# The last row tile of w_ada as TensorE weights in two chunks of the head

## The chip, the cores and the metric

The kernel runs on one core of one Trainium2 chip. The metric is the device time of one launch, in microseconds (us); less is better.

## The reference, cut to what matters

The program is one decoder block on 256 tokens of width 2048, float32 throughout. Before anything else it needs the conditioning vector's projection:

```python
mod = (jax.nn.silu(c) @ w_ada[l] + b_ada[l])[:, None, :]
sh1, sc1, gt1, sh2, sc2, gt2 = jnp.split(mod, 6, axis=-1)
h = rmsnorm(x, g_pre_mix[l]) * (1.0 + sc1) + sh1
y = hybrid_mixer(h, ...)            # h @ w_in, attention heads and recurrent heads, @ w_out
x = x + gt1 * rmsnorm(y, g_post_mix[l])
h = rmsnorm(x, g_pre_ffn[l]) * (1.0 + sc2) + sh2
y = hier_moe(h, ...)                # 32 experts of three 2048 x 512 matrices each
x = x + gt2 * rmsnorm(y, g_post_ffn[l])
```

`c` is one row of 2048 numbers and `w_ada` is 2048 x 12288, so this is a vector times a matrix: all of the matrix is read, and each number is used once. The head of the kernel needs the first two of the six parts, shift `sh1` and scale `sc1`, before `h` exists.

## The kernel before, in words

**The head.** The 2048 columns of shift and scale are cut into five chunks of 4, 4, 4, 2 and 2 tiles of 128 (`CHUNKS`, line 93). A chunk holds the same column tiles of shift and of scale, so a chunk of 4 tiles is 1024 numbers wide. Its 16 row tiles of 128 rows come in four pieces `("head", c, r)` of four row tiles each, and each piece in four transfers: two for its first two row tiles (semaphore `landed`), two for its last two (semaphore `rest_landed`), sent by the SP queue (SyncE) in `head` (from line 370, the DMA itself on line 380). After each chunk's four pieces SP sends blocks of `w_in` (`first`, through `send`, line 361). SP sends in a fixed order written out by hand and waits, in that order, until the ring slot that a piece goes into is free.

**Chunk 0** is done by TensorE as a row product (line 578). **Chunks 1 to 4** are done by VectorE: `head_piece` (from line 1671) runs through the 16 row tiles of the chunk, and for each it does `sum = w_row_tile * silu(c)_tile + sum`, the first on line 1686 and the other 15 on line 1688. The sum is 128 partitions by 1024 (512 for chunks 3 and 4) and still has to be summed over the partitions. After the last piece it raises `part_ready`.

**TensorE's part** is `head_columns(c)`: after `mod_copied` for the chunk before, it issues constant products on fixed data whose result is never read (line 585: 16 in chunk 1, 8 in chunk 2, none in 3 and 4), waits for `part_ready`, and multiplies each 128 x 128 tile of the sum, as weights, with a column of ones (line 598), 8 narrow products for a chunk of 4 tiles, into 8 columns of PSUM bank 7. ScalarE copies these columns to `mod` (line 1287), VectorE makes the affine numbers (lines 1729 to 1731), and VectorE and ScalarE apply them to the chunk's tiles of `hT` (lines 1733 and 1291).

**The order around it.** TensorE is in order. It takes `hT` tile by tile (k = 0 to 15) and multiplies it with 15 column tiles of `w_in` (line 641). Within the last k of chunk c, after 8 of the 15 tiles (1 for chunk 2's last k), it runs `head_columns(c + 1)`. So chunk 1's columns stand inside k = 3, and chunk 2's inside k = 7; the 7 tiles behind them cover the trip through ScalarE and VectorE before k = 4 or k = 8 starts. A slot of the ring is given free by VectorE after it has read a piece (`free` in `head_piece`), and SP may then send the next into it.

**Behind the head** come the rest of the input projection, the recurrent heads, attention, the output projection, the routing, and from about 615 us on the experts, whose weights stream through the ring to the end.

In the profile a float32 product has two rows for each matmul, so 8 narrow products are x16 and 16 constant ones are x32.

Of the kernel before, what the change touches and what calls it, by code (L numbers as in the profile page):

```python
# [34 lines left out]
P = 128  # L35
D = 2048
S = 256
TT = S // P
KT = D // P
# [49 lines left out]
TRANSFERS = [[2 if name[0] == "head" else 1 for name in names] for names in SLOT_LOADS]  # L89
PLACE = {name: (slot, n) for slot, names in enumerate(SLOT_LOADS) for n, name in enumerate(names)}  # L90
HEAD_TILES = 15
IN_ORDER = 16
CHUNKS = [(0, 4), (4, 4), (8, 4), (12, 2), (14, 2)]
BY_DVE = [k0 + i for k0, n in CHUNKS for i in range(n // 2)]
# [84 lines left out]
def block_kernel(nc, a, out):  # L179
# [3 lines left out]
    with ExitStack() as ctx:  # L183
# [5 lines left out]
        def sig(name):  # L189

            if name in STAGE_OF:
                stages, n = STAGE_OF[name]
                counted = sig(stages)
                assert counted.n == n - 1, name
                return counted
            if name not in sems:
                sems[name] = Signal(ctx.enter_context(nc.semaphore(name)))
            return sems[name]

        def wait(eng, name, n=1):  # L200

            if name in STAGE_OF:
                name, n = STAGE_OF[name]
            eng.wait_ge(sig(name).sem, n)
# [20 lines left out]
        silv = sb("silv", [P, KT])  # L225
# [82 lines left out]
        bank = [ctx.enter_context(nc.psum_tensor(f"bank{i}", [P, BLK], F32)) for i in range(8)]  # L308
# [16 lines left out]
        def landed(eng, name):  # L325

            s, n = PLACE[name]
            eng.wait_ge(sig(f"landed{s}").sem, 16 * sum(TRANSFERS[s][0:n + 1]))

        def free(ins, name):  # L330

            ins.then_inc(sig(f"freed{PLACE[name][0]}").sem, 1)
# [17 lines left out]
        def rows_of(name, k, n):  # L350
            return flat(name)[:, 0:k * n].rearrange("p (k c) -> p k c", k=k)
# [3 lines left out]
        def _(sp):  # L355
# [27 lines left out]
            def first(q, h):  # L383
                send(("first", q, h), win_k[:, 4 * q + 2 * h:4 * q + 2 * h + 2, HEAD_COL:HEAD_COL + HEAD_TILES * P])

# [130 lines left out]
            for e in range(2, NE - 2):  # L516
                if e < IN_ORDER:
                    first_halves(e, e % 2)
                for s in range(2, HB):
                    next_piece(e + 1, s, e)  # L520
                if e >= IN_ORDER:
                    first_halves(e, e % 2)
# [25 lines left out]
        def _(pe):  # L548
            mm = nc.tensor.matmul
# [32 lines left out]
            def constant_products(n, first_chunk=False):  # L582

                for _ in range(n):
                    mm(bank[0 if first_chunk else 7][:, S + 64:2 * S], ident, cst[:, C_UP:C_UP + 192], start=first_chunk, stop=True,
                       skip_group_check=True)

            def head_columns(c):

                k0, n = CHUNKS[c]  # L590
                if c > 0:
                    wait(pe, "mod_copied", c)
                    constant_products((16, 8, 0, 0)[c - 1])
                pe.wait_ge(sig("part_ready").sem, c + 1)
                if c == 0:
                    wait(pe, "shift_row")
                for j in range(2 * n):
                    last = mm(bank[7][:, S + 2 * k0 + j:S + 2 * k0 + j + 1], head_sums[c % 2][:, j * P:(j + 1) * P], ones[:, 0:1], start=c == 0, stop=True,
                              skip_group_check=True)
                last.then_inc(sig("column_sums").sem, 1)  # L600

            def late_row(w, out):
# [20 lines left out]
            for c in range(5):  # L623
                k0, nk = CHUNKS[c]
                for k in range(k0, k0 + nk):
                    q, h = k // 4, k % 4 // 2
# [4 lines left out]
                    if k % 2 == 0:  # L631
                        landed(pe, ("first", q, h))
                    w = rows_of(("first", q, h), 2, HEAD_TILES * P)
                    tiles = list(range(HEAD_TILES))
                    if k == KT - 1:
                        tiles = tiles[7:] + tiles[:7]
                    for n, t in enumerate(tiles):
                        if c < 4 and k == k0 + nk - 1 and n == (8, 8, 1, 8)[c]:
                            head_columns(c + 1)
                        half_ = bank[(t - 1) // 2][:, (t - 1) % 2 * S:((t - 1) % 2 + 1) * S] if t else bank[7][:, 0:S]  # L640
                        last = mm(half_, w[:, k % 2, t * P:(t + 1) * P], hT[:, k, :],  # L641
                                  start=k == 0 and (t == 0 or t % 2 == 1), stop=k == KT - 1, skip_group_check=True)
                        if k == KT - 1 and t == HEAD_TILES - 1:
                            last.then_inc(sig("forget_full").sem, 1)
# [5 lines left out]
            for r in range(4):  # L650
                for j in range(4):
                    k = 4 * r + j
                    last = mm(bank[4][32 * j:32 * j + 32, 0:S], wg24[:, k, :], hT[:, k, :], start=r == 0, stop=r == 3,
                              skip_group_check=True)
# [3 lines left out]
            for k in range(KT):  # L658
                last = mm(bank[3][:, 0:S], rows_of("hq", KT, P)[:, k, :], hT[:, k, :], start=k == 0, stop=k == KT - 1)
# [131 lines left out]
            for v, name in enumerate(("w1k", "w1v")):  # L791
# [3 lines left out]
                for r in range(8):  # L795
                    for j in range(4):
                        q = 4 * r + j
                        last = mm(bank[3][32 * j:32 * j + 32, v * P:(v + 1) * P], blkv[:, q, :], rows_of(name, CMP_LEN, P)[:, q, :],
                                  start=r == 0, stop=r == 7, skip_group_check=True)
# [4 lines left out]
            for v in range(2):  # L804
                c0, n = (256, 32) if v == 0 else (288, 160)
                last = mm(bank[3][:, c0:c0 + n], cpart[:, v * P:(v + 1) * P], cst[:, C_SUM:C_SUM + n], start=True, stop=True)
# [4 lines left out]
            last = mm(bank[3][:, 448:480], w2[:, 0, :], cmph[:, 0, 0:32], start=True, stop=True)  # L811
            for g in range(KVG):
                last = mm(bank[3][:, g * P:(g + 1) * P], cmph[:, 1, 16 * g:16 * g + P], w2[:, 1, :], start=True, stop=True)
# [65 lines left out]
            for tt in range(TT):  # L879
                for h in range(NH):  # L880
                    o = bank[3 + 2 * tt + h // 4][:, (h % 4) * P:(h % 4 + 1) * P]
                    for jt in range(tt + 1):
                        aT = at[:, h, tt * P:(tt + 1) * P] if jt == 0 else at[:, h, S:S + P]
                        last = mm(o, aT, htok[:, h // 4, jt, (h % 4) * P:(h % 4 + 1) * P], start=jt == 0, stop=jt == tt)
# [8 lines left out]
            for g in range(KVG):  # L893
                for tt in range(TT):
                    last = tr(bank[1][:, (2 * g + tt) * P:(2 * g + tt + 1) * P], pcp[:, tt, g * P:(g + 1) * P], ident)
# [96 lines left out]
            for tt in range(TT):  # L992
                for m in range(4):
                    wait(pe, "rec_gated", tt * NH + 4 * (m // 2) + 4)
                    for j in range(2):
                        h = 2 * m + j
                        last = tr(bank[OUT_BANKS[2 + tt][m // 2]][:, (m % 2) * 256 + j * P:(m % 2) * 256 + (j + 1) * P],
                                  orec[:, tt, h * P:(h + 1) * P], ident)
# [34 lines left out]
            for m in range(3):  # L1033
                for k in range(4 * m, 4 * m + 4):
                    mm(bank[GB[m]][:, (k % 4) * P:(k % 4 + 1) * P], x_t[:, 0, k * P:(k + 1) * P], onehot[:, 0, :],
                       start=k % 4 == 0, stop=False, skip_group_check=True)
# [9 lines left out]
            last = mm(bank[3][:, 32:64], cst[:, C_UP:C_UP + P], sel[:, 1, :], start=False, stop=True)  # L1046
# [17 lines left out]
            for m in range(3):  # L1064
                for k in range(4 * m, 4 * m + 4):
                    last = mm(bank[GB[m]][:, (k % 4) * P:(k % 4 + 1) * P], x_t[:, 1, k * P:(k + 1) * P], onehot[:, 1, :],
                              start=False, stop=True, skip_group_check=True)
# [143 lines left out]
            with pe.If(over > 0):  # L1211
# [4 lines left out]
                for tt in range(TT):  # L1216
                    for c in range(4):
# [4 lines left out]
                        for j in range(4):  # L1222
                            k = 4 * c + j
                            last = tr(bank[2 + i % 2][:, j * P:(j + 1) * P], x_t[:, tt, k * P:(k + 1) * P], ident)
# [3 lines left out]
                with pe.Fori(0, NE) as e:  # L1228
                    pe.wait_ge(sig("dense_here").sem, e + 1)
                    for tt in range(TT):  # L1230
                        c = e * 2 + tt
                        for s in range(2):
                            for k in range(KT):
                                last = mm(bank[s][:, :], h2T[:, k, tt * P:(tt + 1) * P], ring[:, 2 * (k // 8) + s, k % 8, :],
                                          start=k == 0, stop=k == KT - 1)
                        last.then_inc(sig("dense_gu").sem, 1)
                        pe.wait_ge(sig("dense_hid").sem, c + 1)
                        for f in range(4):
                            last = tr(bank[2][:, f * P:(f + 1) * P], dhid[:, f:4 * P:4], ident)
                        last.then_inc(sig("dense_T").sem, 1)  # L1240
                        pe.wait_ge(sig("dense_T_copied").sem, c + 1)
                        for n in range(4):
                            for k in range(4):
                                wdn = ring[:, 4 + k // 2, :, :].rearrange("p (k a) b -> p k (a b)", k=2)[:, k % 2, :]
                                last = mm(bank[4 + n][:, :], dhidT[:, k * P:(k + 1) * P], wdn[:, n * BLK:(n + 1) * BLK],
                                          start=k == 0, stop=k == 3)
# [412 lines left out]
        def _(dve):  # L1659
# [13 lines left out]
            def head_piece(q, r):  # L1673

                n = 2 * CHUNKS[q][1] * P
                acc_q = head_sums[q % 2][:, 0:n]
                if r == 0 and q > 1:
                    wait(dve, "column_sums", q - 1)
                landed(dve, ("head", q, r))
                w = rows_of(("head", q, r), 4, n)  # L1680
                for k in range(4):
                    if k == 2:
                        wait(dve, f"rest_landed{r}", 32 * (q + 1))
                    c = silv[:, 4 * r + k:4 * r + k + 1]
                    if r == 0 and k == 0:
                        ins = ts(acc_q, w[:, k, :], c, None, ALU.mult)
                    else:
                        ins = stt(acc_q, w[:, k, :], c, acc_q, ALU.mult, ALU.add)
                    if k < 3:
                        step(ins)  # L1690
                    else:
                        free(ins, ("head", q, r))
                        used(dve, ("head", q, r))
                if r == 3:
                    dve.sem_inc(sig("part_ready").sem, 1)
# [271 lines left out]
            for h in range(NH):  # L1967
# [5 lines left out]
                for br in range(2):  # L1973
                    for tt in range(TT):
                        c0, n = (0, P) if tt == 0 else (P, 2 * P)
                        w = probs[:, h % 2, br, c0:c0 + n]
# [17 lines left out]
            for tt in range(TT):  # L1994
                for h in range(NH):
                    n = tt * NH + h
# [241 lines left out]
            with dve.If(over > 0):  # L2238
                for tt in range(TT):
                    ts(x_t[:, tt, :], x_t[:, tt, :], rstd2[:, tt:tt + 1], None, ALU.mult).then_inc(sig("dense_x").sem, 1)  # L2240
                for i in range(8):
                    wait(dve, "dense_xT", i + 1)
                    for j in range(4):
                        k = 4 * (i % 4) + j
# [3 lines left out]
                with dve.Fori(0, NE) as e:  # L2248
                    for tt in range(TT):
                        c = e * 2 + tt  # L2250
# [6 lines left out]
                        for n in range(4):  # L2257
                            w = ysum[:, tt, n * BLK:(n + 1) * BLK]
# [19 lines left out]
            for i in range(8):  # L2278
                dve.wait_ge(sig("scattered").sem, 8 * (NE // 2 - 1) + i + 1)
                c0 = LAST_COLS[i % 4] * BLK  # L2280
                w = ysum[:, i // 4, c0:c0 + BLK]
# [56 lines left out]
```

## Time and profile before

| | |
|---|---|
| median of 3 runs | 1557.26 us (1556.84 to 1557.4) |
| profiled execution, its own time | 1559.59 us |
| its span, first to last instruction | 1557.7 us |
| TensorE busy | 1510.4 us (97%) |
| VectorE busy | 682.2 us (44%) |
| ScalarE busy | 231.6 us (15%) |
| bytes moved, rate over the span | 589.96 MB, 379 GB/s |
| mean granted TensorE clock | 0.995 |

TensorE counts as busy from a matmul's start to its modelled end, so a busy share near 100% says that it was never without an instruction, not that it ran at its peak. The span is 1.9 us shorter than the execution's own time, and that execution is 2.33 us above the median of the runs.

### The profile page before, as it was taken

What the parts mean: (1) busy time and instruction counts of PE and PEld (TensorE: products, weight loads), DVE (VectorE), ACT (ScalarE), POOL (GpSimd) and SP (SyncE); (2) the same over time, 40 slices, a digit from 0 to 9 for tenths busy, and PEclk for the clock granted to TensorE, in tenths of its full rate; (3) what the DMA queues carried; (4) which work ended last, traced back from release to release, by engine and by line L of the source; (5) the groups of instructions that cost most, each with busy time, mean ns of one, the idle gap of its engine ahead of it and who ended that gap; (6) DMA issues with size and microseconds to landing.
All of it is one profiled execution on the core that took longest, in us unless ns stands there. A gap on an engine that the chain in (4) does not pass through costs nothing.

```text
span 1557.7 us, 19266 instructions
## 1 busy us (share of the span) xinstructions
PE 1510.4 (97%) x7980; PEld 811.0 (52%) x7980; DVE 682.2 (44%) x1228; ACT 231.6 (15%) x443; POOL 41.4 (3%) x57
## 2 busy tenths in 40 slices
PE   5999999999999999999999999999999999999996
PEld 2888888855654446444434434434434434434432
DVE  3574767776887636232332332332332322322325
ACT  2100311121322303011010010011010011010003
POOL 1001000000001200000000000000000000000003
PEclk9999999999999999999999999999999999999998
DMA  9999677799878996899999999999999999999993
GB/s 361 397 385 365 259 270 271 280 359 352 305 289 319 364 387 269 364 427 427 428 429 427 429 429 427 429 428 429 398 423 429 428 428 429 428 428 429 427 429 164
DMA packets 102802, 589.96 MB, mean 379 GB/s; under 512 B 6224, under 2 KB 16944, under 8 KB 77408
## 3 DMA queue, kind: packets, MB, share of 16 engines
q1 hardware_dynamic: 100384, 580.93, 91.9%
q0 software_dynamic: 1696, 5.66, 1.1%
q10 hardware_dynamic: 672, 2.66, 0.4%
q8 instruction: 36, 0.59, 0.2%
q14 instruction: 14, 0.11, 0.0%
HBM read 587.07 MB, written 2.16 MB: 378 GB/s over the span
## 4 chain that ended last, share of the span: by engine, by line
PE 66%; DMA 25%; SPq 5%; DVE 2%; issue 1%; ACTq 0%; ACT 0%; DVEq 0%
DMA ring<-in_w_up 22%; PE bank L1165 21%; PE bank L925 7%; PE bank L1198 7%; PE bank L675 5%; SPq L380 5%; PE bank L1079 4%; PE bank L641 4%; PE bank L866 4%; PE bank L1059 3%; PE bank L709 2%; DMA ring<-in_w_ada 2%; PE bank L688 1%; PE bank L691 1%; DMA ring<-in_w_in 1%; PE bank L1090 1%
## 5 line engine op out<-in xcount | busy, mean ns | idle before, releaser
L1165 PE MATMUL bank<-ring,RN 128*64 128x512 f32 x1488 | 330.9, 593 | 9.4 <-DMA ring<-in_w_up 9.4
L1165 PEld LDWEIGHTS bank<-ring,RN 128*64 128x64 f32 x1488 | 106.5, 137 | 223.1 <-issue 199.0
L1198 PE MATMUL bank<-ring,RN 128*64 128x512 f32 x992 | 219.7, 595 | 0.5 <-issue 0.5
L2216 DVE TENSOR_TENSOR RN<-bank,RN 64x512 f32<-64x512 f32 x31 | 21.5, 693 | 376.1 <-ACT RN L1519 376.1
L1198 PEld LDWEIGHTS bank<-ring,RN 128*64 128x64 f32 x992 | 68.9, 137 | 137.4 <-issue 135.6
L2223 DVE COPY RG<-bank 64x512 f32<-64x512 f32 x64 | 44.1, 689 | 196.1 <-PE bank L1198 188.4
L1059 PEld LDWEIGHTS bank<-RN,RX 128*128 128x128 f32 x976 | 111.5, 192 | 13.0 <-issue 13.0
L1059 PE MATMUL bank<-RN,RX 128*128 128x128 f32 x976 | 115.7, 277 | 0.0
L925 PE MATMUL bank<-ring,RT 128*128 128x512 f32 x256 | 113.0, 596 | 0.8 <-DVE RT L2003 0.8
L1165 PE MATMUL bank<-RT,RN 128*64 128x512 f32 x256 | 112.3, 592 | 0.0
L1079 PE MATMUL bank<-RG,RN 128*128 128x512 f32 x240 | 109.5, 599 | 0.0
L2152 DVE TENSOR_SCALAR RN<-bank,aff 128x128 f32<-128x128 f32 x256 | 87.2, 403 | 43.0 <-PE bank L1059 41.1
L1165 PE MATMUL bank<-RH,RN 128*64 128x512 f32 x240 | 105.4, 592 | 0.0
L2189 DVE TENSOR_TENSOR RT<-RT,bank 128x512 f32<-128x512 f32 x112 | 75.7, 687 | 20.5 <-PE bank L1079 18.6
L675 PE MATMUL bank<-RH,ring 128*128 128x256 f32 x384 | 84.0, 380 | 0.0
L1712 DVE SCALAR_TENSOR_TENSOR wide<-ring,silv,wide 128x1024 f32<-128x1024 f32 x60 | 77.0, 1283 | 8.3 <-DMA ring<-in_w_ada 6.5
L675 PEld LDWEIGHTS bank<-RH,ring 128*128 128x128 f32 x384 | 72.6, 190 | 9.9
L1533 ACT ACTIVATE RG<-bank 64x512 f32<-64x512 f32 x64 | 37.9, 592 | 265.5 <-PE bank L1198 259.1
L925 PEld LDWEIGHTS bank<-ring,RT 128*128 128x128 f32 x256 | 47.5, 190 | 57.2 <-issue 56.1
L1519 ACT ACTIVATE RN<-bank 64x512 f32<-64x512 f32 x31 | 18.3, 589 | 391.0 <-PE bank L1165 391.0
L1165 PEld LDWEIGHTS bank<-RT,RN 128*64 128x64 f32 x256 | 35.1, 137 | 72.2 <-issue 72.2
L1079 PEld LDWEIGHTS bank<-RG,RN 128*128 128x128 f32 x240 | 43.4, 191 | 55.2 <-issue 51.6
(395 smaller groups left out, 1472.6 us busy)
## 6 DMA issues: line engine op xcount, KB each, us to landing
ring<-in_w_down SPq DMA_DIRECT2D x64, 2048.0 KB, 15.5
ring<-in_w_up SPq DMA_DIRECT2D x48, 2048.0 KB, 20.9
ring<-in_w_gate SPq DMA_DIRECT2D x47, 2048.0 KB, 17.3
ring<-in_w_ada SPq DMA_DIRECT2D x32, 2048.0 KB, 10.5
ring<-in_w_in SPq DMA_DIRECT2D x18, 2048.0 KB, 9.2
RT<-in_w_gate SPq DMA_DIRECT2D x17, 2048.0 KB, 15.5
RH<-in_w_up SPq DMA_DIRECT2D x16, 2048.0 KB, 20.0
ring<-in_w_ada SPq DMA_DIRECT2D x48, 512.0 KB, 11.6
```

The source lines that it names most:

```text
L380: sp.dma_start(dst[:, j0:j1, m * w:(m + 1) * w], ada_k[:, 4 * r + j0:4 * r + j1, m * D + k0 * P:m * D + k0 * P + w]).then_inc(sig(landing) ...
L641: last = mm(half_, w[:, k % 2, t * P:(t + 1) * P], hT[:, k, :], start=k == 0 and (t == 0 or t % 2 == 1), stop=k == KT - 1, skip_group_chec ...
L675: last = mm(bank[PAIR[name][m // 2]][:, (m % 2) * S:(m % 2 + 1) * S], w[:, m * P:(m + 1) * P], hT[:, k, :], start=k == 0 and m % 2 == 0, s ...
L866: last = mm(bank[2][:, :], hT[:, k, tt * P:(tt + 1) * P], rows_of((name, k // 8), 8, BLK)[:, k % 8, :], start=k == 0, stop=k == KT - 1)
L925: last = mm(bank[OUT_BANKS[n][tt]][:, :], mixed(k)[:, tt * P:(tt + 1) * P], rows_of(("out", n, h), 8, BLK)[:, k % 8, :], start=k == 0, sto ...
L1059: last = mm(bank[GB[m % 3]][:, (k % 4) * P:(k % 4 + 1) * P], x_t[:, tt, k * P:(k + 1) * P], onehot[:, tt, :], start=tt == 0, stop=tt == TT ...
L1079: mm(bank[4 + i % 4][:, :], ohwT[:, tt * P:(tt + 1) * P], rows[:, c * BLK:(c + 1) * BLK], start=True, stop=True).then_inc(sig("scattered") ...
L1165: last = mm(bank[0][64 * s:64 * s + 64, :], tokT[:, k, q * CAP:(q + 1) * CAP], w[:, k % 8, :], start=k == 0, stop=k == KT - 1, skip_group_ ...
L1198: last = mm(bank[2 + n % 2][64 * (n // 2):64 * (n // 2) + 64, :], hidT[:, k * CAP:(k + 1) * CAP], wdn[:, n * BLK:(n + 1) * BLK], start=k = ...
L1712: ins = stt(acc_w, w[:, k, :], c, acc_w, ALU.mult, ALU.add)
L2152: ins = ts(tokT[:, k, :], bank[GB[m % 3]][:, (k % 4) * P:(k % 4 + 1) * P], aff[:, 2, k:k + 1], aff[:, 3, k:k + 1], ALU.mult, ALU.add)
L2189: ins = v.tensor_copy(w, bank[4 + i % 4][:, :]) if first else tt_op(w, w, bank[4 + i % 4][:, :], ALU.add)
```

## The change

In `head_columns` of chunks 1 and 2, TensorE takes the last row tile (row tile 15) of the chunk's eight column tiles straight from the ring as weights, with column 15 of `silu(c)` moving: 8 narrow products into the same 8 columns of bank 7, before the products of the sum with ones, which accumulate onto them. VectorE leaves out its step for that row tile in these chunks. The constant products go from 16 to 10 in chunk 1 and from 8 to 3 in chunk 2. TensorE now waits for the landing of the last piece before it waits for `part_ready`, and it is TensorE's first product of the sum that gives slot 3 free, no longer VectorE. Nothing else is changed.

```diff
+LAST_ROWS_PE = (1, 2)
...
                 if c > 0:
                     wait(pe, "mod_copied", c)
-                    constant_products((16, 8, 0, 0)[c - 1])
+                    constant_products((10, 3, 0, 0)[c - 1])
+                if c in LAST_ROWS_PE:
+                    landed(pe, ("head", c, 3))
+                    wait(pe, "rest_landed3", 32 * (c + 1))
+                    w = rows_of(("head", c, 3), 4, 2 * n * P)
+                    for j in range(2 * n):
+                        mm(bank[7][:, S + 2 * k0 + j:S + 2 * k0 + j + 1], w[:, 3, j * P:(j + 1) * P], silv[:, KT - 1:KT], start=False, stop=True,
+                           skip_group_check=True)
                 pe.wait_ge(sig("part_ready").sem, c + 1)
...
                 for j in range(2 * n):
                     last = mm(bank[7][:, S + 2 * k0 + j:S + 2 * k0 + j + 1], head_sums[c % 2][:, j * P:(j + 1) * P], ones[:, 0:1], start=c == 0, stop=True,
                               skip_group_check=True)
+                    if c in LAST_ROWS_PE and j == 0:
+                        free(last, ("head", c, 3))
...
-                for k in range(4):
+                for k in range(3 if r == 3 and q in LAST_ROWS_PE else 4):
```

## Rows read from the trace of the kernel before

**Rows 1.** Busy tenths of TensorE and DMA in 40 slices, from the page
```profile
PE   5999999999999999999999999999999999999996
...
DMA  9999677799878996899999999999999999999993
```
**Rows 2.** Chain that ended last, experts: start us, us, what
```profile
830.52 21.87 DMA ring<-in_w_up
852.43 7.14 PE bank L1165 x32
```
**Rows 3.** Stretches: length, busy us of each engine (instructions), clock, DMA share, GB/s
```profile
200.00:300.00 100.00, 100.00 (x1043) 86.91 (x1042) 72.37 (x68) 17.20 (x15) 0.00 (x0) 1.00 0.76 282
...
620.00:640.00 20.00, 18.04 (x93) 7.38 (x91) 6.75 (x26) 0.97 (x2) 0.00 (x0) 1.00 0.71 290
```
**Rows 4.** Timeline of TensorE, 28 to 112 us: start us, us, what
```profile
36.36 1.84 PE L598 MATMUL bank<-ones,wide 128*128 128x1 f32 x16
38.06 1.22 PE L585 MATMUL bank<-cst 128*128 128x192 f32 x6
...
62.38 5.36 PE L585 MATMUL bank<-cst 128*128 128x192 f32 x32
68.38 1.95 PE L598 MATMUL bank<-ones,RN 128*128 128x1 f32 x16 [0.63 <-DVEq L1695]
70.19 3.27 PE L641 MATMUL bank<-RH,RT 128*128 128x256 f32 x14
...
96.17 2.76 PE L585 MATMUL bank<-cst 128*128 128x192 f32 x16
99.44 1.95 PE L598 MATMUL bank<-ones,wide 128*128 128x1 f32 x16 [0.51 <-DVEq L1695]
```
**Rows 5.** Timeline of VectorE, 28 to 160 us
```profile
49.49 18.78 DVE L1688 SCALAR_TENSOR_TENSOR RN<-ring,silv,RN 128x1024 f32<-128x1024 f32 x14 [0.64 <-DMA ring<-in_w_ada]
...
80.52 18.81 DVE L1688 SCALAR_TENSOR_TENSOR wide<-ring,silv,wide 128x1024 f32<-128x1024 f32 x14 [0.61 <-DMA ring<-in_w_ada]
...
127.31 11.78 DVE L1688 SCALAR_TENSOR_TENSOR wide<-ring,silv,wide 128x512 f32<-128x512 f32 x15
```
**Rows 6.** Chain that ended last, 30 to 170 us
```profile
53.04 2.57 SPq L380
...
85.25 11.38 DMA ring<-in_w_ada
...
96.73 1.29 DVE wide L1688
...
98.05 1.30 DVE wide L1688
...
124.38 0.79 PE bank L598 x8
...
141.24 0.79 PE bank L598 x8
```
**Rows 7.** DMA issues at 53.0 to 53.5 us: KB, us to landing
```profile
ring<-in_w_ada SPq DMA_DIRECT2D x1, 512.0 KB, 12.5
```
**Rows 8.** DMA issues at 85.5 to 87 us, and SP's timeline there
```profile
RT<-in_w_in SPq DMA_DIRECT2D x1, 1920.0 KB, 14.8
...
86.53 2.58 SPq L361 DMA_DIRECT2D RT<-in_w_in  x2
```
**Rows 9.** Chain that ended last, behind the head
```profile
304.02 13.93 DMA ring<-in_w_ada
```
**Rows 10.** TensorE's timeline, and stretches with its clock (third number from the right)
```profile
22.70 3.64 PE L578 MATMUL bank<-ring,RN 128*32 128x512 f32 x16 [4.00 <-DMA ring<-in_w_ada]
...
21.00:22.00 1.00, 0.00 (x0) 0.00 (x0) 0.25 (x2) 0.60 (x2) 0.00 (x0) 0.94 1.06 389
...
28.00:29.00 1.00, 1.00 (x8) 1.00 (x7) 0.69 (x1) 0.03 (x1) 0.00 (x0) 0.65 1.05 385
...
68.38:70.33 1.95, 1.95 (x17) 1.95 (x18) 0.00 (x0) 0.00 (x0) 0.00 (x0) 1.00 0.99 410
```

## The prediction

> **What bounds the kernel now.** I began with the page's slices. TensorE shows nine tenths in all but the first and the last slice [rows 1], so I asked which parts of that are held up by something else. The DMA engines are also near full, except in nine of the slices 5 to 17. The two long stages therefore have different limits. In the experts the chain alternates: a transfer of 21.87 us, 7.14 us of TensorE, and again [rows 2]. That stage runs as fast as the weights come, and its end is fixed by when it could begin. Between the head and the experts TensorE is the limit: from 200 to 300 us it is busy 100.00 of 100 us, with the DMA engines at 0.76 [rows 3]. The last stretch where the DMA engines are clearly not full is 620 to 640 us, at 0.71 [rows 3]. So whatever TensorE gains in the head should reach the start of the experts' streaming, as long as nothing in between waits for something that did not move.
>
> Next I read the head in TensorE's timeline. Two idle times are put down to VectorE's last step, 0.63 us before chunk 1's narrow products at 68.38 and 0.51 us before chunk 2's at 99.44 [rows 4]. Ahead of each stand the constant products, 5.36 us and 2.76 us, whose results nobody reads. So TensorE stands for about 6.0 and 3.3 us per chunk waiting or filling, and only VectorE's end (chunk 1), or the landing of the last rows plus two VectorE steps (chunk 2), sets when it may go on. In the chain, chunk 2 is plain: the transfer issued at 85.25 takes 11.38 us and lands at 96.63, VectorE takes its last two row tiles from 96.73 and 98.05, and TensorE follows at 99.44 [rows 4, 6].
>
> **The change, part by part.**
>
> *VectorE, one step less.* Fourteen steps take 18.78 us in chunk 1 [rows 5], 1.34 us each with the gap. The last ended at 68.27, and without it the sum is ready at 66.93. TensorE started 0.11 us after VectorE's end before, so it may start at 67.04. In chunk 2 the step at 98.05 goes [rows 6]. The one at 96.73 stays, since it waits for the landing, and ends at 98.02; with the same lag TensorE may start at 98.13.
>
> *TensorE, chunk 1.* A constant product costs 5.36 / 16 = 0.335 us [rows 4]. Ten end at 62.38 + 3.35 = 65.73. Then come the two added waits for the landing. The last transfer of the piece was issued at 53.04 [rows 6] and took 12.5 us [rows 7], so it landed at 65.54, just before. Eight narrow products with weights from the ring are not in the trace. The nearest rows are the eight with ones, of the same shape: 36.36 to 38.06 is 1.70 us, 68.38 to 70.19 is 1.81 us [rows 4]. I take 1.75, since both are rows of just this form. That gives 67.48 for the first product of the sum. This is later than VectorE's 67.04, so TensorE's own work is now the bound and the idle time is gone. Before it was 68.38: **0.90 us gained**. With 1.81 us and 0.1 us for the two waits it is 0.74, with 1.70 it is 0.95.
>
> *A rule against the row.* The row gives 1.70 / 8 = 0.21 us for one narrow product. The Trainium skill, "TensorE: Matmul & The Clock Gate", section "Back-to-back issue gap", gives about 60 cycles for a free size of 1 to 64, 25 ns; as an estimate by that page the 16 rows of eight products would be 0.4 us, and chunk 1 would then be bound by VectorE's 67.04 and gain 1.34 us. The row has the duration, and I use it.
>
> *TensorE, chunk 2.* Its constant products start 0.90 us earlier, at 95.27. Three cost 3 x 2.76 / 8 = 1.04 us [rows 4], to 96.31. The last rows land at 96.63 whatever TensorE does: the DMA queue is full at this time and the transfer was issued at 85.25, so neither the sooner sum nor the later freeing of slot 3 moves it. TensorE waits until about 96.7, as VectorE does. Plus 1.75 is 98.45, later than VectorE's 98.13. Before it was 99.44: **0.99 us gained in all**, not on top of chunk 1. In other words, what followed the landing was two VectorE steps in a row, and is now eight narrow products beside one step. With 1.81 and 0.1 for waits it is 0.83. If the landing came some tenths earlier with the lighter traffic, it would be 1.1.
>
> *The freeing of slot 3.* It moves from VectorE's end, 68.27, to about 67.7, and in chunk 2 from 99.35 to about 98.7. SP sent the next piece's last transfers around 85 [rows 6], far behind the first of these, so nobody waits. I cost it at nothing; its cover is 17 us in chunk 1.
>
> *What must give way behind it.* Chunk 4's VectorE sum ends at 139.09 [rows 5] and TensorE takes it at 141.24 [rows 6]: 2.15 us of slack, and part of VectorE's chain moves up with the columns. For chunk 3 the chain shows TensorE following its own work at 124.38 with no VectorE step ahead [rows 6]. The block of `w_in` for k = 8 is issued at 86.53 and takes 14.8 us [rows 8], landing at 101.33, and TensorE needs it when the seven tiles behind chunk 2's columns are done, 3.27 us by the same seven tiles at 70.19 [rows 4], so at 103.5 even after the move: it covers a move of 1 us. After 160 us nothing but TensorE is on the chain until a transfer issued at 304.02 [rows 9], which TensorE's products release. It moves with them.
>
> *Sum.* -0.99 us at 101 us, carried through. The profiled execution would go from 1559.59 to 1558.6. That execution is 2.33 us above the median of the runs, so the median goes from 1557.26 to 1556.3, or 0.06%.
>
> **The rivals.**
>
> *A: the gain is given back.* If a transfer sent early in a full queue, or the experts' rhythm, is the true clock of the end, then the 1 us becomes idle time. For it: the DMA engines are full in the head and from 640 us on. Against it: 0.76 from 200 to 300 and 0.71 at 620 to 640 [rows 3]; a queue that is empty there cannot carry an old limit through. Time 1557.3.
>
> *B: the clock falls (the slower side).* TensorE's clock went down once early: in an idle time of 4.00 us it fell within 21 to 22 us (granted 0.94 over that stretch), and it came back within 28 to 29 (0.65) [rows 10]. That is some 6.8 us at 1.2 GHz instead of 2.4, worth 3.4 us of TensorE's time at most. Now each chunk has 16 narrow products in a row, some 3.5 us, in which the weight loads are busy but one column moves. If these were taken for idleness, the clock would fall behind chunk 1's columns, in k = 3 and 4. The price is -0.99 + 3.4 = +2.4 for one fall, 1559.7, and -0.99 + 6.8 = +5.8 for one in each chunk, 1563.1. It decides once the stretch of narrow products is long enough, and the longest seen, 1.95 us at 68.38 right behind 0.63 us of idleness, ran at 1.00 [rows 10]. It is now less than twice that, with the idleness gone. The Trainium skill, same page, section "What's actually happening", says the default state is the throttled one and activity releases it, and it leaves open whether such products count. No row here shows 3.5 us of them.
>
> *C: the columns do not move.* If the last rows in fact land so late in chunk 2 that TensorE waits for them and then does narrow products that cost more from the ring, say 2.6 us as two VectorE steps did, nothing is gained: 1557.3. Against it: the form is the same, and both operands lie in SBUF before and after.
>
> **How the numbers follow.** Two tenths of a per cent, 3.1 us, is about what a measurement of this kernel can tell from no change. Chances: forecast 0.79, A 0.09, C 0.02, one fall of the clock 0.04, two falls 0.03, something unseen on the fast side 0.03. Faster by over 0.2% would need 3.1 us, and all filling and waiting that the two chunks lose is 5.9 us less 3.5 us of new products, so it takes something unseen: 0.03. Slower by over 0.2% is the two falls: 0.03. Within: the other four cases, 0.94. The range: the bounds of the gain are 0.83 and 1.1, which gives 1556.2 to 1556.4. The three runs differ by 0.56 us, which I allow on either side, and the same again below, as the experts' rhythm may lock in slightly better: 1555.2. Above it takes in A and C with the same spread: 1558.0.
>
> **What would show it.** Right: chunk 1's narrow products are 32 rows from about 65.8 with no idle time before the second half; in chunk 2 a short wait for a transfer, from 96.3 to 96.7, the sum's products near 98.45, and the k behind them about 1.0 us earlier; the transfer at 304.02 about 1.0 us earlier; and the experts' rows earlier by as much. Wrong: a clock under 1.00 between 66 and 110 us (B); an idle time of TensorE between 100 and 620 us that grew by 1 us (A); narrow products from the ring that take clearly over 1.8 us for eight (C).

## The result: 0.14% slower, where 0.06% faster was forecast

| | before | changed |
|---|---|---|
| median of the runs | 1557.57 us (20 runs, 1555.97 to 1559.37) | 1559.70 us (20 runs, 1554.94 to 1564.23) |
| ratio | | 1.0014, interval 1.0008 to 1.0020 |
| profiled execution, span | 1559.59, 1557.7 us | 1559.61, 1557.8 us |

The two profiled executions took the same time, and the two sets of runs did not. The changed kernel also spreads more than twice as wide: 9.3 us against 3.4.

TensorE's timeline of the changed kernel (start us, us, what); the rows answer to [rows 4]:

```profile
62.18 3.41 PE L586 MATMUL bank<-cst 128*128 128x192 f32 x20
65.43 1.84 PE L600 MATMUL bank<-silv,ring 128*128 128x1 f32 x16
67.13 1.93 PE L606 MATMUL bank<-ones,RN 128*128 128x1 f32 x16
68.92 4.95 PE L651 MATMUL bank<-RH,RT 128*128 128x256 f32 x14
73.71 23.04 PE L651 MATMUL bank<-RH,ring 128*128 128x256 f32 x106
96.59 1.14 PE L586 MATMUL bank<-cst 128*128 128x192 f32 x6
97.56 1.84 PE L600 MATMUL bank<-silv,ring 128*128 128x1 f32 x16
99.27 3.08 PE L606 MATMUL bank<-ones,wide 128*128 128x1 f32 x16
102.21 5.44 PE L651 MATMUL bank<-RH,ring 128*128 128x256 f32 x14
107.49 20.02 PE L651 MATMUL bank<-RH,RT 128*128 128x256 f32 x92
```

In chunk 1 the plan worked: from the start of the constant products to the first product of the sum it is 67.13 - 62.18 = 4.95 us, and it was 68.38 - 62.38 = 6.00. Both idle times are gone. But the seven tiles behind (x14) take 4.95 us against 3.27 before, and in chunk 2 the eight products of the sum take 3.08 us against 1.95 and the seven tiles 5.44 against 3.27. The same instructions take longer. The stretches of the changed kernel say why; the third number from the right is the granted clock, and the two figures after the length are TensorE's matmul and weight-load time:

```profile
66.00:68.00 2.00, 2.00 (x20) 2.00 (x20) 0.41 (x1) 0.00 (x0) 0.00 (x0) 1.00 0.98 407
68.00:70.00 2.00, 2.00 (x13) 1.82 (x13) 0.63 (x4) 0.41 (x2) 0.00 (x0) 0.77 1.00 415
70.00:72.00 2.00, 2.00 (x6) 1.53 (x6) 0.92 (x5) 1.98 (x3) 0.00 (x0) 0.50 1.01 411
72.00:74.00 2.00, 2.00 (x10) 1.72 (x9) 0.00 (x0) 1.96 (x4) 0.00 (x0) 0.88 1.01 389
...
98.00:100.00 2.00, 2.00 (x19) 2.00 (x18) 0.00 (x0) 0.00 (x0) 0.00 (x0) 0.95 1.02 422
100.00:102.00 2.00, 2.00 (x11) 2.00 (x11) 0.00 (x0) 0.00 (x0) 0.00 (x0) 0.50 1.02 422
104.00:106.00 2.00, 2.00 (x6) 1.58 (x5) 0.00 (x0) 0.15 (x1) 0.00 (x0) 0.50 1.08 356
```

Clock 0.50 of 2.4 GHz is the 1.2 GHz level. In chunk 1 it fell behind the 16 narrow products, in chunk 2 among them, and there with matmuls and weight loads both busy in 2.00 of 2.00 us. The kernel before ran at 1.00 in the same places:

```profile
66.00:70.00 4.00, 3.37 (x26) 3.07 (x24) 2.23 (x2) 0.00 (x0) 0.00 (x0) 1.00 1.00 415
70.00:74.00 4.00, 4.00 (x21) 3.56 (x22) 1.54 (x8) 3.09 (x6) 0.00 (x0) 1.00 1.01 403
98.00:102.00 4.00, 3.49 (x26) 3.12 (x25) 1.62 (x5) 0.18 (x1) 0.00 (x0) 1.00 1.02 424
102.00:106.00 4.00, 4.00 (x20) 3.54 (x19) 0.80 (x3) 1.09 (x2) 0.00 (x0) 1.00 1.03 371
```

The time that it cost: the tiles from k = 8 on start at 107.49, 3.13 us later than in the kernel before, whose row is

```profile
104.36 7.93 PE L641 MATMUL bank<-RH,RT 128*128 128x256 f32 x36
```

The first transfer on the chain behind the head is as late, 307.16 against 304.02 [rows 9]. At the start of the experts 2.75 us are left; one wait for a transfer of `w_in` at 353 us is 0.40 us shorter than before and takes up that much. Two rows of the changed kernel's chain of waits (start us, us, what):

```profile
307.16 13.63 DMA ring<-in_w_ada
...
618.69 2.68 PE bank L1076 x24
```

and the second of them in the kernel before:

```profile
615.94 2.68 PE bank L1066 x24
```

That the two spans end alike all the same is due to the stretch behind. From this row to the end of the span the kernel before took 941.8 us in its profiled execution, which was 2.33 us over the median, and the changed one 939.1. The profiles of the experiments below speak for the second: ten of the fourteen, the changed kernel's among them, took 938.8 to 939.7 us here, with starts from 614.98 to 620.33. So the profile of the kernel before is the unusual one. Why its experts took 2.7 us longer stays open.

So the end of one pair of profiles can't carry the comparison, and the start of the experts carries it better: 2.75 us late there, and 2.1 us at the median.

A second measure is the mean granted clock that every run reports. In 105 runs of the kernel before, made beside the experiments below, it averages 0.9959 (median 1557.69 us), and in the 20 runs of the changed kernel 0.9935. The difference, 0.0024 x 1557 = 3.7 us, is what TensorE would lose if all of it fell where TensorE is the limit. The mean does not say where the clock fell, and places outside the head are in it, as the last section shows. It tells how much of this there was, and not what it cost.

### The profile page after: what moved, and what is told of

It is laid out like the page before. It is cut to its first block, busy times and chain, and to the rows that moved or that the text cites. A ratio compares the mean times of both kernels' runs of the same rounds, so it can differ in the third digit from the quotient of the medians.

```text
span 1557.8 us, 19286 instructions
## 1 busy us (share of the span) xinstructions
PE 1514.3 (97%) x7990; PEld 815.1 (52%) x7990; DVE 679.6 (44%) x1226; ACT 231.6 (15%) x443; POOL 41.3 (3%) x57
## 4 chain that ended last, share of the span: by engine, by line
PE 77%; DMA 20%; DVE 2%; issue 0%; SPq 0%; ACTq 0%; ACT 0%; DVEq 0%
PE bank L1175 22%; DMA ring<-in_w_up 17%; PE bank L1208 9%; PE bank L935 7%; PE bank L651 7%; PE bank L685 5%; PE bank L1069 4%; PE bank L1089 4%; PE bank L876 4%; DMA ring<-in_w_ada 2%; PE bank L719 2%; PE bank L698 1%; PE bank L701 1%; DMA ring<-in_w_in 1%; PE bank L1100 1%; PE bank L842 1%
```

## Experiments

Each kernel was run beside the kernel before. "Clock" is the mean over its runs of each run's mean granted clock. The averages of 11 or 12 runs are uncertain by some 0.0005. In the profiled execution with four tiles between, the clock falls only at the very end, where TensorE is done, and its mean is 0.998.

| kernel | runs | median us | ratio to before, interval | clock |
|---|---|---|---|---|
| before | 105 | 1557.69 | | 0.9959 |
| changed | 20 | 1559.70 | 1.0014 (1.0008 to 1.0020) | 0.9935 |
| all constant products kept | 5 | 1562.93 | 1.0041 (1.0028 to 1.0054) | 0.9940 |
| spare narrow products | 11 | 1560.82 | 1.0017 (1.0008 to 1.0027) | 0.9934 |
| 3 constant products between | 6 | 1561.66 | 1.0026 (1.0014 to 1.0037) | 0.9930 |
| 3 tiles between | 12 | 1557.22 | 1.0005 (0.9994 to 1.0017) | 0.9951 |
| before, fewer constant products | 11 | 1559.13 | 1.0008 (0.9999 to 1.0017) | 0.9938 |
| change in chunk 1 alone | 11 | 1558.32 | 1.0006 (0.9997 to 1.0015) | 0.9950 |
| change in chunk 2 alone | 11 | 1559.26 | 1.0009 (1.0001 to 1.0018) | 0.9946 |
| groups of four | 12 | 1559.52 | 1.0018 (1.0008 to 1.0027) | 0.9942 |
| 4 tiles between | 12 | 1556.97 | 0.9999 (0.9991 to 1.0008) | 0.9959 |
| chunk 2 alone, 4 tiles between | 11 | 1556.20 | 0.9994 (0.9985 to 1.0003) | 0.9956 |
| the same again | 12 | 1556.68 | 0.9993 (0.9984 to 1.0001) | 0.9964 |
| before, columns later | 11 | 1558.05 | 1.0004 (0.9995 to 1.0013) | 0.9942 |

### Is it the constant products that were taken away?

```diff
-                    constant_products((10, 3, 0, 0)[c - 1])
+                    constant_products((16, 8, 0, 0)[c - 1])
```

> The changed kernel with all 16 and 8 constant products kept. Theory N (16 narrow products in a row are what lets the clock fall): the granted clock is 0.5 for some us behind chunk 1's or chunk 2's columns here too, and the time is over that of the changed kernel's full-clock case by the five to six extra products and up to 5 us: 1559 to 1564 us, ratio to before 1.001 to 1.003. Theory F (the missing constant products are what lets it fall): clock 1.00 from 60 to 110 us, the sum's columns in chunk 1 start at 62.3 + 5.4 + 1.7 = 69.4 against 68.4 before, so 1 to 2 us slower than before and no more, with mean clocks as before (0.995 or above).

Measured: 1562.93 us, clock 0.9940. With every constant product in place the clock still fell. In the profiled execution it stayed up behind chunk 1 and went down behind chunk 2, as these stretches show (columns as above):

```profile
102.00:104.00 2.00, 2.00 (x16) 1.86 (x16) 0.42 (x4) 0.20 (x2) 0.00 (x0) 0.93 1.00 394
104.00:106.00 2.00, 2.00 (x6) 1.64 (x5) 0.72 (x2) 1.08 (x2) 0.00 (x0) 0.50 1.05 348
```

Theory F alone is out, since it had the clock at 1.00 throughout. The median is within N's 1559 to 1564 us, the ratio above N's 1.003. These are five runs.

### Is it the ring as the source of weights, or what VectorE no longer does?

```diff
+                if c in (1, 2):
+                    for j in range(2 * n):
+                        mm(bank[7][:, S + 2 * KT + j:S + 2 * KT + j + 1], ident, ones[:, 0:1], start=False, stop=True,
+                           skip_group_check=True)
```

> The kernel before with 10 and 3 constant products and then eight narrow products of an identity tile with a column of ones into unused columns; VectorE does all its steps, and nothing reads the ring for the new products. Theory N or F: the clock falls as in the changed kernel (0.5 behind chunk 1 or 2), and the time is about 1 us above the changed kernel, 1560 to 1562 us median, mean clocks 0.992 to 0.994. Theory W (weights from the ring, or the moving column of silu, have to do with it): clock 1.00 at 60 to 110 us and a time within 1 us of before, since TensorE only fills idle time.

Measured: 1560.82 us, clock 0.9934, the changed kernel's 0.9935. TensorE's stream is that of the changed kernel but for 0.35 us of idleness in chunk 1, and nothing is gained from it. Theory W is out: eight narrow products on fixed data are enough. The median is 1.1 us above the changed kernel's, but runs that range over 7 to 9 us in both don't show this difference (the ratios are 1.0017 and 1.0014), so it is no measure of what the useful part of the change brings.

### Is it 16 narrow products in a row?

```diff
-                    constant_products((10, 3, 0, 0)[c - 1])
+                    constant_products((7, 0, 0, 0)[c - 1])
...
+                    constant_products(3)
                 pe.wait_ge(sig("part_ready").sem, c + 1)
```

> The changed kernel with the same number of constant products, but three of them between the two groups of narrow ones (7+3 and 0+3). Theory N: the clock stays at 1.00 from 60 to 110 us; the sum's columns start at about 68.1 and 99.3, so the time is within 0.5 us of before, and mean clocks are as before. Theory F: the clock falls as in the changed kernel, 1559 to 1562 us.

Measured: 1561.66 us, clock 0.9930. The clock fell behind both chunks in the profiled execution; one stretch behind each:

```profile
70.00:72.00 2.00, 2.00 (x9) 1.63 (x9) 1.25 (x7) 1.06 (x3) 0.00 (x0) 0.60 0.98 400
...
102.00:104.00 2.00, 2.00 (x9) 2.00 (x10) 0.06 (x1) 0.18 (x1) 0.00 (x0) 0.50 0.99 391
```

The longest row of narrow products here is eight, as before. Theory N is out as worded. In chunk 1 TensorE was also idle for 0.64 us ahead of the first group; in chunk 2 it was not idle at all, so idleness is not needed for the fall.

### Real work between the two groups

`head_columns` is cut in two; the sum's part is called three tiles later.

```diff
+                        if c < 4 and k == k0 + nk - 1 and n == (11, 11, 1, 8)[c]:
+                            head_sum_columns(c + 1)
```

> The changed kernel with the sum's columns three tiles of w_in later (after 11 of 15 tiles and not after 8), so that real work stands between the two groups of narrow products. Theory N: clock 1.00 from 60 to 110 us, the sum's columns of chunk 2 start at 99.7 and k = 8 about 1.1 us earlier than before: ratio 0.9985 to 1.000, median about 1556.5 us. Theory F: the clock falls still, and it is not faster than before.

Measured: 1557.22 us, clock 0.9951. The median is 2.5 us under the changed kernel's, and by the ratio it is no faster than before: four of its 12 runs took over 1560 us, the other eight 1555.37 to 1558.38. In the profiled execution the clock held behind chunk 1 and fell in chunk 2, where TensorE had come early with its three constant products and was idle before the narrow ones, as its timeline shows:

```profile
96.46 2.20 PE L601 MATMUL bank<-silv,ring 128*128 128x1 f32 x16 [0.63 <-DMA ring<-in_w_ada]
98.53 2.91 PE L659 MATMUL bank<-RH,ring 128*128 128x256 f32 x6
```

This neither bears out N nor F. It led to theory L: idleness and narrow products count alike.

### Idleness in place of narrow products

```diff
-                    constant_products((16, 8, 0, 0)[c - 1])
+                    constant_products((10, 3, 0, 0)[c - 1])
```

This is the kernel before, with no product added.

> The kernel before with 10 and 3 constant products and nothing else changed: TensorE is idle for about 2.6 and 2.1 us ahead of the sum's eight narrow products, and idle plus narrow make some 4.5 us with hardly a column moved. Theory L (what lets the clock fall is a stretch with few columns moved, be it idleness or narrow products): the clock falls about as often as in the changed kernel, mean clock near 0.9935, median 1559 to 1561 us. Theory N (only narrow products in a row, 1.95 us here as before): mean clock 0.996 as before and the median within 0.5 us of before.

Measured: 1559.13 us, clock 0.9938, nearly that of the changed kernel. TensorE was idle 2.94 us and then did eight narrow products, and the clock fell there. TensorE's timeline:

```profile
68.48 3.37 PE L598 MATMUL bank<-ones,RN 128*128 128x1 f32 x16 [2.94 <-DVEq L1695]
```

and the stretch behind:

```profile
70.00:74.00 4.00, 4.00 (x15) 3.55 (x16) 1.54 (x8) 1.59 (x4) 0.00 (x0) 0.50 0.99 393
```

As L has it. It also shows what the constant products are for: nobody reads their results, and with 11 fewer of them the mean clock is lower and the median 1.4 us higher. The ratio's interval begins at 0.9999, so the clock is shown and the time only likely.

### One chunk alone

`LAST_ROWS_PE = (1,)` with constant products (10, 8), and `(2,)` with (16, 3).

> The change in chunk 1 alone. Theory L: falls behind chunk 1 in most runs, none more than before behind chunk 2; mean clock 0.9945 to 0.995, median 0.5 to 2 us above before. If the falls cost nothing, the gain of chunk 1 alone is 0, since chunk 2 then waits for the same landing: median as before.

Measured: 1558.32 us, clock 0.9950.

> The change in chunk 2 alone. Theory L: falls behind chunk 2 in most runs, mean clock 0.9945 to 0.995, median 0.5 to 2 us above before; in runs of mean clock 0.997 or more, about 0.5 us less than before, since TensorE now goes on from the landing after one VectorE step. Without a cost of the clock, the median would be 0.3 to 0.5 us under before.

Measured: 1559.26 us, clock 0.9946. In either profiled execution the clock fell behind the changed chunk alone. The losses of clock, 0.0009 and 0.0013, add up to 0.0022, against 0.0024 for both, so either chunk has a share of about half, as far as averages this uncertain can tell. The two best runs of the second took 1555.70 and 1556.60 us at a clock of 0.996, where the 33 runs of the kernel before with this clock average 1558.04; two runs are no more than a hint of the gain.

### Four groups of four, with a tile between

The 16 products stand in four groups after tiles 8, 9, 10 and 11, with 10 and 5 constant products ahead.

```diff
+                        if c < 2 and k == k0 + nk - 1 and n in range(8, 12):
+                            narrow_step(c + 1, n - 8)
```

> The changed kernel with the 16 narrow products of a chunk in four groups of four, with one tile of w_in (0.43 us of full-width work) between any two, and 10 and 5 constant products. TensorE's work is the same but for two products. Theory L: a stretch of 3.4 us now holds 1 us or more of full-width work, against none in the changed kernel, so the clock falls seldom: mean clock 0.996, median 1.0 to 1.4 us under before (1556.4 to 1556.8), ratio about 0.9992. Theory C (the clock falls by some chance that has nothing to do with how the narrow products stand): mean clock 0.9935 and slower than before by 1 to 3 us.

Measured: 1559.52 us, clock 0.9942. A miss for L with the measure that I had put to it: with a tile of full-width work between any two groups of four the mean clock was nearly that of the changed kernel, and far from the 0.996 expected. The last groups of chunk 1 and what followed, in TensorE's timeline:

```profile
67.81 0.68 PE L675 MATMUL bank<-RH,RT 128*128 128x256 f32 x2
68.32 0.95 PE L605 MATMUL bank<-ones,RN 128*128 128x1 f32 x8
69.13 0.68 PE L675 MATMUL bank<-RH,RT 128*128 128x256 f32 x2
69.64 1.09 PE L605 MATMUL bank<-ones,RN 128*128 128x1 f32 x8
70.60 3.51 PE L675 MATMUL bank<-RH,RT 128*128 128x256 f32 x8
```

and the stretch with the clock:

```profile
70.00:72.00 2.00, 2.00 (x9) 1.75 (x9) 0.94 (x5) 0.73 (x3) 0.00 (x0) 0.58 1.00 407
```

The four tiles at 70.60 took 3.51 us; the same tiles at full clock take 1.97.

### Two groups, four tiles apart and next to no idleness

The sum's part stands after 12 tiles instead of 8, with 10 and 5 constant products.

> The changed kernel with four tiles of w_in (1.74 us) between the two groups of narrow products and 10 and 5 constant products, so that TensorE is not idle while it waits for chunk 2's last rows. Theory L (the clock falls when a stretch with few columns moved is long): each narrow group of 1.75 us now has full-width work on both sides, less than the 0.6 us of idleness and 1.95 us of narrow products of before; mean clock 0.9955 or more, median 1556.6 to 1557.2 us, 0.5 to 1.2 under before. Theory T (it is the total of narrow products near each other that counts, however parted within 6 us): mean clock 0.994 to 0.995 as in the variant with four groups of four, 1558 to 1560 us.

Measured: 1556.97 us, clock 0.9959, that of the kernel before. In the profiled execution the clock did not fall in the head at all; one of the 12 runs had 0.992 and took 1561.64 us, so falls are rarer here, and not gone. TensorE's timeline at chunk 1:

```profile
65.61 1.92 PE L601 MATMUL bank<-silv,ring 128*128 128x1 f32 x16 [0.20 <-DMA ring<-in_w_ada]
67.39 1.97 PE L659 MATMUL bank<-RH,RT 128*128 128x256 f32 x8
69.20 1.84 PE L611 MATMUL bank<-ones,RN 128*128 128x1 f32 x16
70.90 1.54 PE L659 MATMUL bank<-RH,RT 128*128 128x256 f32 x6
```

and the two stretches with their clock:

```profile
66.00:70.00 4.00, 4.00 (x30) 3.79 (x30) 0.86 (x1) 0.00 (x0) 0.00 (x0) 1.00 1.02 424
98.00:102.00 4.00, 4.00 (x31) 3.79 (x30) 0.00 (x0) 0.00 (x0) 0.00 (x0) 1.00 1.02 422
```

TensorE does the same 16 narrow products here as in the changed kernel, and the median is 2.7 us lower. Theory T's clock and time are both missed. The three tiles left behind the sums, 1.54 us, cover the way through ScalarE and VectorE: k = 4 follows at 72.28 with no idle time. What the change was to gain is seen here, since the clock is out of the way. Work on k = 8 starts 0.93 us before the 104.36 of the kernel before:

```profile
103.43 8.84 PE L659 MATMUL bank<-RH,RT 128*128 128x256 f32 x40
```

and the experts' first row on the chain starts 0.96 us earlier, at 614.98 against 615.94. At the medians of the runs this gain does not show: the ratio is 0.9999, with 0.9991 to 1.0008.

### Chunk 2 alone, four tiles apart

Chunk 1 is as before. Chunk 2 has 2 constant products, the narrow group on the last row tile, four tiles, the sum's group and three tiles.

> The change in chunk 2 alone, 2 constant products there and four tiles of w_in between the two narrow groups; chunk 1 as before with 16. Theory L: mean clock 0.9955 or more and median 0.3 to 1.0 us under before (1556.7 to 1557.4), since the wait for chunk 2's landing is what the gain hangs on. Theory T: a fall behind chunk 2 in half of the runs, mean clock about 0.995, and the median at or above before.

Measured: 1556.20 us, ratio 0.9994 (0.9985 to 1.0003), clock 0.9956. This is the best version, and it was run once more:

> The same kernel as the variant with the change in chunk 2 alone and four tiles between its narrow groups, for a second interval. If its gain is real, the ratio is again 0.9990 to 0.9998 and the median about 0.9 us (0.3 to 1.5) under before, with a mean clock of 0.9955 to 0.9965; if the first interval was luck, the ratio is 1.0000 to 1.0006.

Measured: 1556.68 us, ratio 0.9993 (0.9984 to 1.0001), clock 0.9964. Over both, 23 runs have a median of 1556.65 us, 1.0 under before's 1557.69. It beats the changed kernel clearly. Against the kernel before, both ratios lie in the expected range, but each interval still reaches 1, so a gain of 0.06% is likely and not proved. In both profiled executions the clock fell behind chunk 1, whose code is before's, and the seven tiles there took 4.96 us: so the kernel before has such falls too, at times.

### Only the order changed, in the kernel before

```diff
-                        if c < 4 and k == k0 + nk - 1 and n == (8, 8, 1, 8)[c]:
+                        if c < 4 and k == k0 + nk - 1 and n == (11, 11, 1, 8)[c]:
```

with 12 constant products for 16 in chunk 1.

> The kernel before, nothing taken from VectorE, with the chunk's narrow products after 11 of 15 tiles instead of 8 in chunks 1 and 2, and 12 constant products for 16 in chunk 1 (8 in chunk 2 as before): three tiles of real work stand ahead of VectorE's end and not behind it. No narrow product is added, so under L and T alike the clock does as before (0.996). The four tiles left behind the columns, 1.74 us, cover the 1.1 us through ScalarE and VectorE. Expected 1.3 us earlier at k = 8, median 1556.2 to 1556.6 us, ratio 0.9990 to 0.9996. If the four tiles do not cover it, or the fewer constant products cost clock, as before or slower.

Measured: 1558.05 us, clock 0.9942: a miss. Three tiles did come ahead of VectorE's end, but the mean clock is lower (0.9942, where the runs of before beside it had 0.9961), with no narrow product added. In chunk 2 of the profiled execution TensorE was idle 0.87 us and the four tiles behind took 3.16 us in place of 1.97, by its timeline:

```profile
99.17 1.95 PE L598 MATMUL bank<-ones,wide 128*128 128x1 f32 x16 [0.87 <-DVEq L1695]
100.97 3.16 PE L641 MATMUL bank<-RH,ring 128*128 128x256 f32 x8
```

## Why the prediction was wrong

**VectorE, one step less: right.** In chunk 1 its 13 steps end at 66.42 in the changed kernel, before TensorE's 67.13, and TensorE no longer waits.

**TensorE, chunk 1: right.** Eight narrow products with weights from the ring start 1.70 us ahead of the next group (65.43 to 67.13); I had taken 1.75. From the start of the constant products chunk 1 gained 1.05 us, with 0.90 forecast. The estimate by the Trainium skill, "TensorE: Matmul & The Clock Gate", section "Back-to-back issue gap", 0.4 us for the eight, was off by four times. The same section says that this gap is a matmul's by itself, and that it comes out too small at small free sizes where each matmul has a weight load; I had left that out. Here each of the 16 rows has a weight load (192 ns on average in the changed kernel's profile, each overlapping the next), and the rows follow each other every 0.106 us.

**TensorE, chunk 2: right, but not seen in the changed kernel.** There TensorE came late from chunk 1's fall of the clock, began the narrow products at 97.56 and had no landing to wait for. With three tiles between, where it came early, it waited 0.63 us for the transfer and went on at 96.46; I had taken about 96.7.

**The freeing of slot 3: nobody waited**, as costed. The last rows of chunk 2 had landed before TensorE came to them at 97.56.

**The sum, "carried through": right as a mechanism.** With four tiles between, where the clock held in the profiled execution, k = 8 came 0.93 us earlier and the experts 0.96 us, with 0.99 forecast, and from there on ten profiles took the same time within 1 us. The changed kernel's 3.13 us at k = 8 came through as 2.75. So rival A (given back) has at most these 0.4 us for it. At the medians the gain itself is not shown: no ratio below 1 has an interval that leaves 1 out. The one run of the changed kernel with a mean clock of 0.998 took 1554.94 us, the lowest of its 20. Rival C (dear narrow products) is out by the 1.70 us.

**The step that failed is the price of narrow products**, which I took for their own 1.75 us only; the sum has no term for the clock. I gave rival B, the fall of the clock, 7 in 100, and dismissed it with one row: 0.63 us of idleness and 1.95 us of narrow products had run at 1.00 [rows 10]. Three things were wrong in this. One execution shows one outcome of something that varies from run to run: before's 105 runs range from 0.994 to 0.998 in mean clock, and two profiles of code that is before's in chunk 1 show the fall that its own profile lacks. The row was the most that had been shown to pass, and the change went beyond it, so it spoke for doubt and not for safety. And I read the constant products as waste, "waiting or filling", where taking 11 of them away took the mean clock from 0.9959 to 0.9938. B's mechanism and its place were as described. Its price of 3.4 us a fall was an upper bound: in the profiled execution the two falls cost 1.69 us (from 68.92 to 73.71, where the same tiles took 3.10 before) and 3.3 us (from 97.56 to 107.49, 9.93 us, where eight ring products, the eight of the sum and the seven tiles take 1.71 + 1.81 + 3.11 at full clock). At the median, with all that the change gained, it came to +2.1 us, and not to +2.4 or +5.8.

One figure of the prediction does not come out of its rows. The "5.9 us" of filling and waiting that the two chunks lose is 4.9 (6.00 - 3.35 in chunk 1 and 3.27 - 1.04 in chunk 2). Less 3.5 us of new products that leaves 1.4 us, so that a gain of 3.1 us was further out of reach than stated.

The Trainium skill, "TensorE: Matmul & The Clock Gate", section "What's actually happening", has activity release the throttle. The runs agree in that the clock came back while the tiles of `w_in` ran (0.88 at 72 to 74 us). Whether products of one column are such activity it leaves open. In this case the clock fell while TensorE did nothing but these, its matmuls busy in 2.00 of 2.00 us.

**What stays open** is the rule itself. Four tiles between the groups held the clock as well as before; one tile between groups of four did not, nor did three constant products, and three tiles with 0.63 us of idleness did in part. Three tiles (0.9951) and four tiles (0.9959) are not told apart by 12 runs each, and the version with four also had less idleness and two more constant products, so which of these helped is not shown. The later columns with 12 constant products ahead did not hold it. All of it is compatible with "too little full-width work around the gap", but these runs don't give a measure of it, and none was made to find one.

## What to carry to other kernels

Matmuls that move one column keep TensorE busy in the profile, but here they took the clock down as idle time did (mean 0.9934 with spare ones added, 0.9938 with idle time in their place). So count them as a gap, together with the idle time beside them, before replacing filler work (here the constant products) by them. If such products must be added, put full-width work between the groups and leave little idleness next to them: that is the one arrangement here that kept the mean clock with 16 of them. Where the clock is at stake, compare mean granted clocks over ten or more runs, and look in the profiles for where it falls. The span of a single profile, and even of a pair, told nothing here.

## What the runs showed of the hardware

- With matmuls and weight loads both busy for 2.00 of 2.00 us, the granted clock still fell to 0.50 (stretch of 100 to 102 us of the changed kernel). A busy share is no assurance of the clock.
- Such a fall is a matter of chance in the same program: behind chunk 1, with the same code in chunk 1, the clock held in the profile of the kernel before and fell in both profiles of the version with chunk 2 alone and four tiles between. The 20 runs of the changed kernel have mean clocks from 0.992 (seven runs, 1559.54 to 1564.23 us) to 0.998 (one run, 1554.94 us).
- The fall after the early idle time of 4.00 us, on which I had priced rival B [rows 10], is there in seven of the fourteen profiles and absent from the other seven, the changed kernel's among them. Though it lasts some 7 us, it costs next to nothing: chunk 1's constant products start at 61.97 to 62.38 us with it and at 61.85 to 62.65 without it. It takes some 0.002 off a run's mean clock all the same.
- The clock also fell in code that no version changes. In the profiles of the spare narrow products and of the kernel before with fewer constant products it went to 0.50 near 644 and 641 us, behind idle times of 1.44 and 0.52 us that the kernel before has too, at 1.00. The 32 products there took 8.35 and 8.73 us, where the kernel before took 7.09. These are the slowest executions of the two versions, 1564.75 and 1561.73 us. How often this happens in a run of either kernel is not known, so a part of the 2.1 us may lie there and not in the head.
